# Output projections of a two-block transformer, divided along the contraction

## The chip, the cores and the metric

One core of a Trainium2 chip runs the whole program. The metric is the device time of one execution in microseconds (us). The engines are named as in the profile: PE is TensorE (matmul), PEld its weight load, DVE is VectorE, ACT is ScalarE, POOL is GpSimd, SP is SyncE.

## The reference

256 tokens of width 1024 go through four layers. All weights are float32 and are read once. The part that matters here is how each layer's attention output gets to its output projection:

```python
# first block, two layers
q, k, v, qi, ki, wi, u, vs = split(x @ w_in[i])
a_out = dsa_attention(...)            # top-64 keys chosen by an index score, 8 heads of 64 -> 512 columns
b_out = gelu(u) * (w_s @ layer_norm(gelu(vs)) + b_s)           # "gating", 512 columns
x = layer_norm(ALPHA * x + concatenate([a_out, b_out]) @ w_o[i])
# ... then ple gate, SwiGLU feed-forward, layer_norm

# second block, layer 0 (even) and layer 1 (odd)
o = concatenate([o_a, o_b])   # even: MLA 512 + dilated 256 columns; odd: differential 512 + MoBA 512
x = x + g1 * (o @ w_out)      # then rms_norm, modulate, squared-relu MLP, x + g2 * ...
```

## The kernel before

The 256 tokens are two tiles of 128 (`t` = 0, 1). A weight matrix comes in as a row of items of up to 128x2048 elements (1 MB); an item of 1024 rows x 512 columns is four contraction blocks of 128 rows. SP loads items into three buffers `RAW`; ACT rounds an item into `WH` and DVE subtracts to get `WL` (a **split**, done by `advance()`, at most `NPAIR` = 3 split items ahead of the items used up). The activations are turned on PE and split in the same way into `XTH`/`XTL` (`to_XT`, `turn_halves`: transposes on PE, then ACT writes XTH, then DVE writes XTL). A product is then three matmuls of 128x512 for each block (lines 1355 to 1357), so one whole item costs 12 matmuls for each token tile.

The order of work is written out once, as a list of parts (`do(...)`), and each engine runs its own share of every part strictly in the order of that list. A part that has to wait on an engine therefore holds up every later part on that engine. `busy(b, n)` (line 1340) puts `n` bf16 matmuls of 128x512 whose result is thrown away (**pads**) in front of a part; `pad`, `pads` and `first` set their number.

`attention(units, scale, filler, steps, pads, first)` runs over units of a few heads. Step k issues the scores of unit k, the transposes of unit k-1 (2 pads ahead unless said otherwise), then `steps[k]` pieces of a generator `filler`, then the products with the values for unit k-2. Softmax lies between: DVE reduces, ACT takes exponentials.

Before the attention of the first block stands the **selection**: PE index scores, then eight rounds on DVE (`sel_round`: MAX8 and MATCH_REPLACE8 for both tiles, lines 1834 and 1837) and the mask `selb` (line 1844), for which the first scores wait. In between, `next(fill)` issues the four items of `w_in` that give u and vs. They run on PE beside the rounds, in the order u, vs; ACT applies gelu into `GB`. After the last round comes `sgu_ln`, the layer norm of vs: two sums and two squares on ACT, small steps on POOL, two applications on ACT, then two multiplications and two additions of 128x512 on POOL (lines 1307 and 1311). The gating (8 matmuls and 4 DVE operations for each of two halves, lines 1411 and 1907, with a mask of the weights on DVE, line 1899) is a filler of the first three steps of the attention.

The output projection: in the attention, as soon as the attention output of tile 0 is ready, all of its 1024 (even layer: 768) columns are turned, and tile 0 is multiplied with the first 512 output columns. Then `guard` holds the rest until the attention is over. The other three of the four products (column half c, tile t) follow with the full contraction: (0,1), (1,0), (1,1). Behind each, DVE adds it to X (`residual`, or `gated_put`, two operations). The first block then normalises (`ln_tile`: statistics on DVE, two small steps on POOL, two operations on DVE) and runs `w_ple` and `w_ple_gate`; the second does `norm_tile` (ACT, POOL, DVE) and `go(t)` (8 transposes, modulation on ACT and DVE, split) before `mlp_w1`, which stands behind 11 pads.

Of the kernel before, what the change touches and what calls it, by code (L numbers as in the profile page):

```python
# [22 lines left out]
ALPHA = 4 ** 0.25  # L23
# [20 lines left out]
def plan():  # L44

    out = []

    def all_rows(name, i, k, *cuts):
        for cols in cuts:
            out.append((name, i, (0, k), cols if isinstance(cols, list) else [cols]))  # L50
# [18 lines left out]
    for i in range(2):  # L69
        if i == 0:  # L70
# [6 lines left out]
            all_rows("even_w_out_2", 0, 768, *halves)  # L77
        else:
# [3 lines left out]
            all_rows("odd_w_out_2", 0, 1024, *halves)  # L82
# [92 lines left out]
def program(nc, W, xd, xTd, pTd, posd, pos2d, colvd, cstd, cstbd, vecd, sgwd, smalld, out):  # L175
    with ExitStack() as ctx:
# [72 lines left out]
        def stationary(name, kt, t):  # L249
            if name == "x":  # L250
                return XTH[:, kt, tok(t)], XTL[:, kt, tok(t)]
            if name == "p":
                return PTH[:, kt, tok(t)], PTL[:, kt, tok(t)]
# [175 lines left out]

        def run(gen):  # L430
            for _ in gen:
                pass
# [57 lines left out]
        def to_XT(src, n, after, t, pad=0):  # L490
            return turn_halves([src[:, t, k * 128:k * 128 + 128] for k in range(n)], after, XTH, XTL, t, pad)
# [122 lines left out]
        def ln_tile(key, t, after, between=None):  # L614
            sts, mv = col(12), col(2)
            do("ln_stats", key, t, sts, mv, after)
            do("rsqrt", ("ln", key), mv[:, 1:2], 1.0, 1e-5, ("ln_mv", key))
            if between:
                between()
            do("ln_apply", key, t, mv)  # L620
            return [("ln", key)]
# [31 lines left out]
        for i in range(2):  # L653
# [21 lines left out]
            gw = [[], []]  # L675

            def gelus():
                for c in range(2):
                    def put(t, b, done, c=c):
                        do("gelu", (i, c, t), t, c, b, [done] + gb_free)  # L680
                        gw[t].append(("gelu", (i, c, t)))
                        give(b, gw[t][-1])
                    yield from linear("w_in", "x", xt_w, put)

            fill = gelus()
# [19 lines left out]
            for rnd in range(8):  # L705
# [4 lines left out]
                if rnd % 2:  # L710
# [4 lines left out]
            do("sgu_ln", i, gw, [col(1) for _ in range(2)], [col(1) for _ in range(2)], [col(1) for _ in range(2)],  # L715
               list(sq["free"]))
            sq["free"] = [("ln_ss", (i, 1))]
            vsw = [("sgu_ln", (i, t)) for t in range(2)]
# [23 lines left out]
            def gating():  # L742
                yield
                do("sgw_mask", i)
# [1403 lines left out]
```

How the kernel before makes its waits and increments, by code:

```python
    def wait_ge(self, sem, value):  # L169
        if self.past.get(id(sem), 0) < value:
            self.eng.wait_ge(sem, value)
            self.past[id(sem)] = value
# [1066 lines left out]
        def sync_program(eng):  # L1239
            on = Waits(eng)
            def load(n):
                it = seq[n]
                w = it["n"] * it["w"]
                if n >= NRAW:
                    on.wait_ge(*at(*seq[n - NRAW]["freed"]))
                eng.dma_start(RAW[:, n % NRAW, 0:w], W[it["off"]:it["off"] + 128 * w].rearrange("(p w) -> p w", p=128)
                              ).then_inc(*landed(f"raw{n % NRAW}", n))
            for n in range(NRAW):
                load(n)
            eng.dma_start(X[:, :, :], xd[0].rearrange("(t p) d -> p t d", p=128)).then_inc(*landed("x", 0))
            for n in range(NRAW, len(seq)):
                load(n)
            for part, args in order:
                if part == "store":
                    t, after = args
                    for e in after:
                        on.wait_ge(*at(*e))
                    eng.dma_start(out[0, tok(t), :], X[:, t, :]).then_inc(*landed(f"out{t}", 0))
            for t in range(2):
                on.wait_ge(*at(f"out{t}", 0))
# [11 lines left out]
            def rsqrt(key, x, scale, eps, summed):  # L1274
                on.wait_ge(*at("cst", 0))
                on.wait_ge(*at(*summed))
                eng.tensor_scalar(x, x, scale, eps, ALU.mult, ALU.add).then_inc(*own.up())
                on.wait_ge(*own.at())
```

## Time and profile before

| | |
|---|---|
| time, median of 3 runs | 1501.52 us (1497.39 to 1505.88) |
| the profiled execution | 1503.37 us, of which the span (first to last instruction) 1501.6 us |
| mean granted PE clock | 0.968 of 2.4 GHz |
| PE busy | 1414.2 us (94%) |
| DVE busy | 949.5 us (63%) |
| ACT busy | 657.9 us (44%) |
| POOL busy | 108.9 us (7%) |
| DMA | 269.87 MB, mean 180 GB/s |
| chain that ended last, by engine | PE 77%, DVE 13%, ACT 4%, issue 3%, DMA 2%, POOL 2% |

Times inside the profile are in us from the span's start. "Busy" counts an engine's own instructions, pads included. A matmul's duration overlaps the next one, so what a run of matmuls costs is the distance between their starts. The granted clock is a share of 2.4 GHz: 1.00 is 2.4 GHz, 0.50 is 1.2 GHz.

### The profile page before, as it was taken

What the parts mean: (1) busy time and instruction counts of PE and PEld (TensorE: products, weight loads), DVE (VectorE), ACT (ScalarE), POOL (GpSimd) and SP (SyncE); (2) the same over time, 40 slices, a digit from 0 to 9 for tenths busy, and PEclk for the clock granted to TensorE, in tenths of its full rate; (3) what the DMA queues carried; (4) which work ended last, traced back from release to release, by engine and by line L of the source; (5) the groups of instructions that cost most, each with busy time, mean ns of one, the idle gap of its engine ahead of it and who ended that gap; (6) DMA issues with size and microseconds to landing.
All of it is one profiled execution on the core that took longest, in us unless ns stands there. A gap on an engine that the chain in (4) does not pass through costs nothing.

```text
span 1501.6 us, 16677 instructions
## 1 busy us (share of the span) xinstructions
PE 1414.2 (94%) x6765; PEld 1140.7 (76%) x6765; DVE 949.5 (63%) x1239; ACT 657.9 (44%) x886; POOL 108.9 (7%) x156
## 2 busy tenths in 40 slices
PE   6999999999998999998799898999998998899998
PEld 6767888887867888886789666788876666688886
DVE  4856777766756677765586636766665775544444
ACT  4544533333554443433455334454435434355442
POOL 1010000001020000000222200000003120000000
PEclk9989999999999999999999869999999998999999
DMA  8504688863613688872243104677763330345451
GB/s 331 189 15 188 225 294 300 296 234 128 228 41 134 228 311 293 284 272 77 102 168 113 43 0 162 247 279 261 260 219 132 120 112 1 123 161 186 177 194 56
DMA packets 40236, 269.87 MB, mean 180 GB/s; under 512 B 4544, under 2 KB 4688, under 8 KB 11872
## 3 DMA queue, kind: packets, MB, share of 16 engines
q1 hardware_dynamic: 37712, 259.31, 48.2%
q0 software_dynamic: 2304, 8.46, 1.6%
q8 instruction: 53, 0.87, 0.2%
q10 hardware_dynamic: 144, 1.05, 0.2%
q14 instruction: 23, 0.19, 0.0%
HBM read 267.75 MB, written 1.05 MB: 179 GB/s over the span
## 4 chain that ended last, share of the span: by engine, by line
PE 77%; DVE 13%; ACT 4%; issue 3%; DMA 2%; POOL 2%; SPq 0%; POOLq 0%; DVEq 0%; ACTq 0%
PE ps L1355 21%; PE ps L1357 20%; PE ps L1356 20%; PE ps L1380 4%; PE ps L1432 4%; DVE WL L1662 3%; DMA RAW<-W 2%; PE ps L1447 2%; PE ps L1340 2%; ACT WH L1460 1%; PE ps L1368 1%; PE ps L1434 1%; POOL st L1279 1%; DVE SCR L1837 1%; DVE st L1924 1%
## 5 line engine op out<-in xcount | busy, mean ns | idle before, releaser
L1662 DVE TENSOR_TENSOR WL<-RAW,WH 128x2048 fp32r<-128x2048 f32 (+5 forms) x210 | 453.3, 2161 | 279.9 <-ACT WH L1460 279.7
L1355 PE MATMUL ps<-WH,XTH 128*128 128x512 f32 (+3 forms) x1176 | 460.6, 392 | 32.7 <-DVE XTL L1667 14.0
L1460 ACT ACTIVATE WH<-RAW 128x2048 fp32r<-128x2048 f32 (+5 forms) x210 | 379.9, 1810 | 247.0 <-PE ps L1357 219.5
L1357 PE MATMUL ps<-WH,XTL 128*128 128x512 f32 (+3 forms) x1176 | 449.3, 382 | 0.0
L1356 PE MATMUL ps<-WL,XTH 128*128 128x512 f32 (+3 forms) x1176 | 448.4, 381 | 0.0
L1355 PEld LDWEIGHTS ps<-WH,XTH 128*128 128x128 f32 x1176 | 223.7, 190 | 76.3 <-DVE XTL L1667 14.2
L1357 PEld LDWEIGHTS ps<-WH,XTL 128*128 128x128 f32 x1176 | 223.4, 190 | 38.8
L1356 PEld LDWEIGHTS ps<-WL,XTH 128*128 128x128 f32 x1176 | 223.7, 190 | 37.0 <-issue 1.9
L1355 PE MATMUL ps<-WH,HTH 128*128 128x512 f32 (+1 forms) x452 | 179.6, 397 | 3.2 <-DVE HTL L1743 3.2
L1356 PE MATMUL ps<-WL,HTH 128*128 128x512 f32 (+1 forms) x452 | 178.7, 395 | 0.0
L1357 PE MATMUL ps<-WH,HTL 128*128 128x512 f32 (+1 forms) x452 | 178.6, 395 | 0.0
L1721 DVE SCALAR_TENSOR_TENSOR ACC<-RAW,colv,ACC 128x512 f32<-128x512 f32 x168 | 126.1, 751 | 5.1
L1355 PEld LDWEIGHTS ps<-WH,HTH 128*128 128x128 f32 x452 | 85.9, 190 | 22.8 <-DVE HTL L1743 3.7
L1460 ACT ACTIVATE HTH<-ps 128x512 fp32r<-128x512 f32 (+1 forms) x58 | 32.1, 586 | 160.5 <-PE ps L1380 160.3
L1357 PEld LDWEIGHTS ps<-WH,HTL 128*128 128x128 f32 x452 | 85.9, 190 | 19.7
L1356 PEld LDWEIGHTS ps<-WL,HTH 128*128 128x128 f32 x452 | 86.1, 190 | 19.2
L1277 POOL TENSOR_SCALAR st<-st 128x1 f32<-128x1 f32 (+3 forms) x42 | 21.6, 514 | 1073.0 <-DVE st L1927 547.2
L1460 ACT ACTIVATE E<-ps,st 128x128 f32<-128x128 f32 (+1 forms) x104 | 42.5, 419 | 112.0 <-DVE st L1866 112.0
L1460 ACT ACTIVATE GB<-ps 128x512 f32<-128x512 f32 (+1 forms) x94 | 46.4, 499 | 88.3 <-PE ps L1357 88.1
L1340 PE MATMUL ps<-cstb 128*128 128x512 bf16 x283 | 81.7, 412 | 0.0
L1432 PE MATMUL ps<-T 64*128 64x128 f32 (+3 forms) x208 | 71.4, 435 | 8.7 <-DVE selb L1844 4.4
L1743 DVE TENSOR_TENSOR HTL<-ps,HTH 128x512 fp32r<-128x512 f32 x54 | 35.8, 687 | 37.7 <-ACT HTH L1460 37.7
(175 smaller groups left out, 1124.0 us busy)
## 6 DMA issues: line engine op xcount, KB each, us to landing
RAW<-W SPq DMA_DIRECT2D x220, 1024.0 KB, 4.8
RAW<-W SPq DMA_DIRECT2D x7, 960.0 KB, 4.7
RAW<-W SPq DMA_DIRECT2D x6, 910.0 KB, 5.8
RAW<-W SPq DMA_DIRECT2D x9, 576.0 KB, 3.5
VEC<-vecd POOLq DMA_DIRECT2D x10, 512.0 KB, 6.1
RAW<-W SPq DMA_DIRECT2D x8, 512.0 KB, 3.3
RAW<-W SPq DMA_DIRECT2D x6, 546.0 KB, 4.3
GB<-xTd ACTq DMA_DIRECT2D x1, 1024.0 KB, 8.4
```

Of the source, the lines that this page charges most:

```text
L1277: eng.tensor_scalar(x, x, scale, eps, ALU.mult, ALU.add).then_inc(*own.up())
L1340: eng.matmul(banks[b][:, :], identb, cstb[:, 0:512], start=True, stop=True)
L1355: eng.matmul(ps, xh, hi[:, j, c0:c0 + cw], start=first and j == 0, stop=False)
L1356: eng.matmul(ps, xh, lo[:, j, c0:c0 + cw], start=False, stop=False)
L1357: op = eng.matmul(ps, xl, hi[:, j, c0:c0 + cw], start=False, stop=last and j == n - 1)
L1380: op = eng.transpose(banks[b][0:rows, j * 128:j * 128 + 128], src, ident)
L1432: op = eng.matmul(banks[b][:, c:c + nk], q, ks, start=True, stop=True)
L1447: op = eng.matmul(banks[b][:, c0:c0 + dv], PET[:, u["i"], blk * 128:blk * 128 + 128], val, start=(j == 0), stop=(j == len(lst) - 1))
L1460: return eng.activation(dst, src, f, **k)
L1662: eng.tensor_tensor(WL[:, p, 0:w], RAW[:, n % NRAW, 0:w], WH[:, p, 0:w].bitcast(F32), ALU.subtract).then_inc(*up("wl", n))
L1721: op = eng.scalar_tensor_tensor(out=ACC[:, a, :], in0=view[:, j, :], scalar=cond[:, kt:kt + 1], in1=ACC[:, a, :], op0=ALU.mult, op1=ALU.add)
L1743: eng.tensor_tensor(HTL[:, r2:r2 + 2, :], banks[b][:, :].rearrange("p (n q) -> p n q", n=2), HTH[:, r2:r2 + 2, :].bitcast(F32), ALU.subtra ...
```

## The change

The contraction of every output projection is cut in two halves, each with its own item order in `plan()` and its own evacuation. In the first block, half one is the gating's 512 columns; in the second it is the 512 columns of the attention that ran earlier. Its four products are fillers of the attention from the second step on. The other half is done for tile 0 inside the attention, and for tile 1 behind it. Each of the four (c, t) results is therefore added to X twice: `residual` and `gated_put` run 8 times in a layer, not 4.

So that the gating's columns are there when the attention starts, vs comes before u in `w_in`, `sgu_ln` is divided in three parts (`sgu_sum`, `sgu_square`, `sgu_ln`), and mask and gating are pieces of the same filler as the gelus, of which now every round but the first takes one, not every second. The statistics of tile 0's layer norm are taken inside the attention. The pads change: 8 ahead of the first unit's transposes in the first block become 3, `first` in its second layer becomes 6.

```diff
@@ plan()
-        all_rows("w_in", i, 1024, (0, 364), (364, 728), (728, 1092), (1092, 1604), (1604, 2116))
-        all_rows("w_o", i, 1024, *halves)
+        all_rows("w_in", i, 1024, (0, 364), (364, 728), (728, 1092), (1604, 2116), (1092, 1604))
+        some_rows("w_o", i, 512, 1024, *halves)
+        some_rows("w_o", i, 0, 512, *halves)
...
-            all_rows("even_w_out_2", 0, 768, *halves)
+            some_rows("even_w_out_2", 0, 0, 512, *halves)
+            some_rows("even_w_out_2", 0, 512, 768, *halves)
...
-            all_rows("odd_w_out_2", 0, 1024, *halves)
+            some_rows("odd_w_out_2", 0, 0, 512, *halves)
+            some_rows("odd_w_out_2", 0, 512, 1024, *halves)
@@ new
+        def slots(its, lhs, after, evac, steps, pad=0):
+            for c, t in steps:
+                advance()
+                it, (b, fr), g = its[c], take(), uid()
+                do("mm", it, t, lhs, [(b, 0, it["w"], (g, t))], True, True, after[t], fr, 0 if c else pad)
+                if t:
+                    cur["used"] += 1
+                evac(c, t, b, ("mm", (g, t)))
+                flush()
+                yield
@@ first block, selection
             def gelus():
-                for c in range(2):
...
-                    yield from linear("w_in", "x", xt_w, put)
-
-            fill = gelus()
+                yield from gelu(1)
+                do("sgu_sum", i, gw, sgu[0], list(sq["free"]))
+                yield
+                second = gelu(0)
+                next(second)
+                do("sgu_square", i, sgu[0], sgu[1], sgu[2])
+                sq["free"] = [("ln_ss", (i, 1))]
+                yield
+                run(second)
+                do("sgu_ln", i, sgu[1], sgu[2])
+                do("sgw_mask", i)
+                yield
...
+            def gating():
+                for gh in range(2):
+                    b, fr = take()
+                    do("gating", i, gh, b, vsw + fr)
+                    give(b, ("gated", (i, gh)))
+                    yield
+
+            fill = chain(gelus(), gating())
...
-                if rnd % 2:
+                if rnd:
                     next(fill, None)
@@ first block, attention and behind it
             def out_start():
+                for t in range(2):
+                    mg[t][:] = to_XT(MIX, 8, [sgo], t, k0=4)
+                yield
+                yield from slots(two("w_o"), "x4", mg, put_gated, ((0, 0), (0, 1), (1, 0), (1, 1)))
                 while "out" not in keys_[0]:
                     yield
-                mo[0][:] = to_XT(MIX, 8, [keys_[0]["out"], sgo], 0)
+                mo[0][:] = to_XT(MIX, 4, [keys_[0]["out"]], 0)
                 yield
-                yield from linear("w_o", "x", mo, put_o(0), touter=True, guard=lambda: tail["go"], pad=(0, 3),
-                                  mid=lambda: mo[1].extend(to_XT(MIX, 8, [keys_[1]["out"], sgo], 1, pad=3)))
-
-            fill = chain(gating(), out_start())
-            attention(units, 0.125, fill, pads=(8,), first=8 if i else 3)
+                its_o.extend(two("w_o"))
+                yield from slots(its_o, "x", mo, put_o, ((0, 0), (1, 0)))
+                ln.append(ln_start((i, 1, 0), 0, rw[0]))
+                yield
+            fill = out_start()
+            attention(units, 0.125, fill, (1, 1, 2, 1, 1, 1, 1, 1), pads=(3,), first=6 if i else 3)
...
-            run(linear("w_o", "x", mo, put_o(1), touter=True,
-                       mid=lambda: x_n.__setitem__(0, ln_tile((i, 1, 0), 0, rw[0]))))
+            x_n[0] = ln_end(*ln[0])
+            mo[1][:] = to_XT(MIX, 4, [keys_[1]["out"]], 1, pad=3)
+            run(slots(its_o, "x", mo, put_o, ((0, 1), (1, 1)), pad=3))
+            xt_n[0][:] = to_XT(X, 8, x_n[0], 0)
             x_n[1] = ln_tile((i, 1, 1), 1, rw[1])
@@ second block, attention and behind it
             def out_start():
+                for t in range(2):
+                    xo[t][:] = to_XT(MIX, 4, [keys_[t]["out"]], t)
+                yield
+                yield from slots(two(nm_out), "x", xo, put_1, ((0, 0), (0, 1), (1, 0), (1, 1)))
                 while "out" not in keys_[2]:
                     yield
...
+                xo2[0][:] = to_XT(MIX, n_out, [keys_[2]["out"]], 0, k0=4)
                 yield
...
+                its_o.extend(two(nm_out))
+                yield from slots(its_o, "x4", xo2, put_2, ((0, 0), (1, 0)))
...
-            attention(units, 0.125, fill, first=3 if i else 0)
+            attention(units, 0.125, fill, (1, 1, 2, 1, 1, 1, 1, 1) if i else 1, first=3 if i else 0)
...
+            norm_tile(0, xg[1][0])
+            xo2[1][:] = to_XT(MIX, n_out, [keys_[3]["out"]], 1, pad=2, k0=4)
+            rest = slots(its_o, "x4", xo2, put_2, ((0, 1), (1, 1)), pad=3)
+            next(rest)
+            go(0)
+            run(rest)
+            norm_tile(1, xg[1][1])
```

## Rows read from the trace of the kernel before

**Rows 1.** Page, section 5: DVE's half of a split; busy, mean ns | idle before, releaser.

```profile
L1662 DVE TENSOR_TENSOR WL<-RAW,WH 128x2048 fp32r<-128x2048 f32 (+5 forms) x210 | 453.3, 2161 | 279.9 <-ACT WH L1460 279.7
```

**Rows 2.** Waits of PE: engine, line, releaser: us in total, times, longest.

```profile
PE ps L1380 <- DVE MIX L1942: 11.0, 5, 3.7
...
PE ps L1432 <- DVE selb L1844: 4.4, 2, 2.7
```

**Rows 3.** Windows: length, busy (x count) of PE, PEld, DVE, ACT, POOL, PEclk, DMA share, GB/s.

```profile
72.80:85.00 12.20, 12.17 (x44) 7.63 (x44) 4.87 (x7) 7.53 (x23) 7.09 (x9) 0.58 0.02 8
85.00:108.30 23.30, 23.30 (x143) 17.97 (x143) 12.12 (x24) 8.33 (x22) 0.00 (x0) 1.00 0.07 23
...
418.90:429.80 10.90, 10.86 (x45) 6.93 (x45) 5.21 (x7) 7.46 (x23) 7.08 (x10) 0.69 0.05 18
...
858.00:890.00 32.00, 32.00 (x112) 20.69 (x112) 9.10 (x30) 8.29 (x35) 0.00 (x0) 0.50 0.00 1
890.00:904.10 14.10, 14.10 (x96) 11.71 (x95) 6.78 (x11) 5.28 (x12) 0.00 (x0) 1.00 0.14 38
...
1249.30:1262.00 12.70, 12.70 (x47) 8.02 (x47) 4.91 (x10) 4.52 (x21) 1.21 (x2) 0.60 0.00 1
```

**Rows 4.** Timeline, first layer's selection and gating: start, us, engine, line, operation [idle before].

```profile
72.83 0.48 PE L1432 MATMUL ps<-T 64*128 64x128 f32 x2 [2.74 <-DVE selb L1844]
...
56.56 0.62 DVE L1834 MAX8 st<-SCR 128x8 f32<-128x128 f32 x2
...
57.74 0.61 DVE L1834 MAX8 st<-SCR 128x8 f32<-128x128 f32 x2
...
80.42 1.22 DVE L1899 TENSOR_TENSOR T<-T,cst 128x1024 f32<-128x1024 f32 x1
...
85.18 1.13 DVE L1907 SCALAR_TENSOR_TENSOR MIX<-ps,colv,GB 128x128 f32<-128x128 f32 x4 [3.55 <-PE ps L1411]
...
69.47 0.60 ACT L1460 ACTIVATE GB<-ps 128x512 f32<-128x512 f32 x1 [2.12 <-PE ps L1357]
...
74.83 2.49 POOL L1307 TENSOR_TENSOR GB<-GB,VEC 128x512 f32<-128x512 f32 x2
77.28 2.94 POOL L1311 TENSOR_TENSOR GB<-GB,VEC 128x512 f32<-128x512 f32 x2
```

**Rows 5.** Timeline of PE, first layer: pads, turned output, matmuls of w_o, gate.

```profile
79.37 3.62 PE L1340 MATMUL ps<-cstb 128*128 128x512 bf16 x8
...
109.52 1.09 PE L1380 MATMUL ps<-cst,MIX 128*128 128x128 f32 x8 [0.37 <-DVE MIX L1893]
...
112.27 0.47 PE L1355 MATMUL ps<-WH,XTH 128*128 128x512 f32 x1 [1.02 <-DVE XTL L1739]
...
115.11 0.39 PE L1355 MATMUL ps<-WH,XTH 128*128 128x512 f32 x1
...
117.83 0.39 PE L1355 MATMUL ps<-WH,XTH 128*128 128x512 f32 x1
...
142.64 0.50 PE L1355 MATMUL ps<-WH,XTH 128*128 128x512 f32 x1 [1.11 <-DVE WL L1662]
```

**Rows 6.** Timeline of DVE, first layer: layer norm of tile 1.

```profile
135.31 1.28 DVE L1924 BATCH_NORM_STATS2 st<-X 128x6 f32<-128x512 f32 x2
...
139.10 1.28 DVE L1937 SCALAR_TENSOR_TENSOR X<-X,st,VEC 128x1024 f32<-128x1024 f32 x1
```

**Rows 7.** Groups of PE by form in the even layer's attention, 855:890, then 890.1:905.

```profile
L1432 PE MATMUL ps<-T 64*128 64x256 f32 x18 | 11.0, 710 | 0.0
...
L1432 PE MATMUL ps<-T 64*128 64x256 f32 x6 | 2.1, 428 | 0.0
```

**Rows 8.** Timeline of PE, even layer: mlp_w1 starts, tile 1 is turned.

```profile
927.21 0.49 PE L1355 MATMUL ps<-WH,XTH 128*128 128x512 f32 x1 [2.89 <-DVE XTL L1768]
...
932.17 1.09 PE L1380 MATMUL ps<-cst,MIX 128*128 128x128 f32 x8
```

More of the change, by code:

```diff
@@ L488, in turn_halves, with to_XT @@
             return outs
-        def to_XT(src, n, after, t, pad=0):
-            return turn_halves([src[:, t, k * 128:k * 128 + 128] for k in range(n)], after, XTH, XTL, t, pad)
+        def to_XT(src, n, after, t, pad=0, k0=0):
+            return turn_halves([src[:, t, k * 128:k * 128 + 128] for k in range(k0, n)], after, XTH[:, k0:n, :],
+                               XTL[:, k0:n, :], t, pad)
         def col(n):
@@ L674, in program, with gelu, put @@
             do("load_vec", i, 1, VEC[:, 1024:2048], vb + 1024, vec_free[1])
-            gw = [[], []]
-            def gelus():
-                for c in range(2):
[L679 to L682, printed above, removed]
-                    yield from linear("w_in", "x", xt_w, put)
-            fill = gelus()
+            gw = []
+            sgu = [[col(1) for _ in range(2)] for _ in range(3)]
+            def gelu(c):
+                def put(t, b, done):
+                    do("gelu", (i, c, t), t, c, b, [done] + gb_free)
+                    if c:
+                        gw.append(("gelu", (i, c, t)))
+                    give(b, ("gelu", (i, c, t)))
+                return linear("w_in", "x", xt_w, put)
+            def gelus():
+                yield from gelu(1)
[10 more added lines that the diff above has]
+                yield
+            vsw = [("sgu_ln", (i, t)) for t in range(2)]
+            sgo = ("gated", (i, 1))
+            def gating():
[5 more added lines that the diff above has]
+            fill = chain(gelus(), gating())
             for t in range(2):
@@ L740, in program @@
                                           blocks=[c * 128 for c in range(per * (t + 1))]))
-            def gating():
-                yield
-                do("sgw_mask", i)
-                for gh in range(2):
-                    b, fr = take()
-                    do("gating", i, gh, b, vsw + fr)
-                    give(b, ("gated", (i, gh)))
-                    yield
-            sgo = ("gated", (i, 1))
             rw = [[], []]
             x_o, x_n = x_w, [None, None]
-            mo = [[], []]
@@ L885, in gain, with gated_put @@
             give(b, ("gain", g))
-        def gated_put(layer, c, k, xg):
-            def put(t, b, done):
-                do("gated_put", (layer, k, c, t), t, c, k, b, [done] + vg_w[k] + (xo_w[t] if k == 0 else []), x_w[t])
-                vg_free[k] = [("gp", (layer, k, c, t))]
-                xg[t].append(("gx", (layer, k, c, t)))
-                give(b, ("gp", (layer, k, c, t)))
-            return put
+        def gated_put(layer, k, buf, xg, c, t, b, done, after, x_after):
+            key, v = (layer, k, c, t), k // 2
+            do("gated_put", key, t, c, v, buf, b, [done] + vg_w[v] + after, x_after)
+            vg_free[v] = [("gp", key)]
+            xg[t].append(("gx", key))
+            give(b, ("gp", key))
         def put_H(name, c, a, b_, lst):
@@ L1214, in last @@
                 for c in range(2):
-                    gated_put(i, c, 1, xg)(t, acc4[t][c][0], done[c])
+                    gated_put(i, 2, MIX, xg, c, t, acc4[t][c][0], done[c], [], x_w[t])
                 if t:
```

96 lines of the change are left out of this document (50 added, 46 removed).

## The prediction

> **What bounds the kernel now.** I read four views, in this order. The page first: PE is busy for 94% of the span and 77% of the chain that ended last is PE, so the question for every edit is what PE waits for and what it does that is no work. The waits of PE say where it stands idle: behind MIX of the second block's norms, and for the selection mask [rows 2]. The windows of the stages this change touches are the most telling. In all of them PE is busy in practically every microsecond, through the softmax too, so there is no hole in the attention into which matmuls could be put for nothing [rows 3]. And they show the granted clock: 0.58 and 0.69 where the first block's attentions begin, 0.50 for 32 us in the even layer's attention, 0.60 where the odd one's begins. Last the timelines, for the order on each engine.
>
> **What is moved, and its price.** Twelve 128x512 matmuls, one item for one tile, cost 2.72 us at 2.4 GHz (117.83 less 115.11) [rows 5], 0.227 each. Of the 96 matmuls of an output projection 24 run in the attention now and 72 behind it; after the change it is 72 and 24. That is 48 matmuls or 10.9 us from one side to the other, in the even layer 42 or 9.5 us. As PE has no hole, I count this as neutral. Gains and losses are in the waits, the pads and the clock.
>
> **First block, selection: +9.5 us in each of two layers.** The gating now stands in the order in front of round 6, and its DVE half in front of rounds 6 and 7, so DVE cannot finish the selection before PE has done the gating, and PE cannot before POOL has normalised vs. Taken by the first layer:
> - ACT still does the gelus of the last item (now u) when PE ends it, 69.47 and 0.60 [rows 4]. `sgu_ln` stands behind them on ACT: two operations, the first done at about 70.8.
> - POOL then has its four operations, 2.49 + 2.94 us for the pairs [rows 4], or 4 x 1.25 = 5.0 if the additions are not disturbed. It ends at 75.9 to 76.3.
> - DVE reaches the gating after the weight mask (1.22) and round 5, near 71.5 (a round is 57.74 less 56.56, 1.18) [rows 4], and stands still.
> - PE's half of the gating takes 1.4 us at 1.2 GHz (PE idle by then for 6 us), DVE's 1.13, then round 6 (1.18), the second gating (1.13), round 7 (1.18) and the mask (0.3): 76.0 + 1.4 + 0.2 + 4.9 = 82.4. The scores began at 72.83 [rows 4]. Behind the waiting DVE instruction are queued the two last rounds and the mask; behind PE's are all scores.
>
> Bounds: 8.5 (POOL undisturbed, gating at 2.4 GHz) to 11. The removal of 2.3 us of gating from the attention is counted below. The sums and squares, done earlier, cost nothing: ACT waits for PE there.
>
> **First block, up to the third unit's scores: +4 and +5 us.** Now 12.2 and 10.9 us [rows 3]. Eight pads (3.4 from 79.37 on, at 1.2 GHz [rows 5]) and half of the gating (1.4) go. Three pads (1.3), eight transposes at 1.2 GHz (1.7) and 12 matmuls come. After an idle time of nearly 10 us with only the gating in it PE starts at 1.2 GHz, in the second layer too, so scores that ran fast cost 1 and 2 us more. What brings the clock back? Before, it was back within 5 us of the first of the 8 pads; I take the same from the new pads and matmuls on, so 12 matmuls cost 4.7. That gives 16.1 in both. Bounds: -3 (never cold) to +6.
>
> **First block, rest of the attention: +6.9 us each.** This stretch has 24 matmuls of w_o now and 60 then: +36, or +8.2; less the second half of the gating (0.9) and 4 transposes (0.4). The 23.3 us [rows 3] become 30.2. The extra DVE work (four residuals of 0.7, two turned halves, two splits of 2.2 [rows 1]) lies beside: DVE is busy for 12.12 of 23.3 us [rows 3]. Uncovered, it would cost 2 us in a step.
>
> **First block, behind the attention: -10.4 and +0.5 us each.** Now from 108.3 to the last matmul of w_o: PE waits until 112.27 (4.0) and does 72 matmuls (16.3), 20.3 in all [rows 5]. After: the transposes start as now (109.52), half of them, but on DVE the two operations of tile 0's norm (1.28 each [rows 6]) stand ahead of XTL, so PE starts at 4.4, and 24 matmuls end at 9.9. Behind it `slots` has no closing `advance()`: the first item of w_ple_gate is split on DVE behind the norm of tile 1. XTL of X at 2.6, the norm as now from 135.31 to 140.38 (5.1) [rows 6], the split 2.2: at 9.9. PE has only 6.3 us of work until then and stands for 3.6; then 12 matmuls, 4 pads and 8 transposes to 14.4, against 14.0 now (to 142.64 [rows 5]).
>
> One layer of the first block: 9.5 + 4 (5) + 6.9 - 10.4 + 0.5, about +10.5 and +11.5, **+22 us**.
>
> **Even layer: -13 us.** In its attention PE ran at 1.2 GHz for 32 us without a pause [rows 3]. The same scores cost 710 ns there and 428 ns behind it [rows 7], so this stretch is 0.6 as long at 2.4 GHz, or, with the pads and transposes, which halve, 0.57. The change puts 12 dense matmuls into the second step, about 858, and 24 more behind them. If they act like the pads of the first block [rows 5], the clock is up at 863; what came before from 856.6 on (34.8 us up to the last but two steps) then takes 19.6. Added are 30 matmuls more (6.8). The attention ends near 902, where it was 904.1: -2, with 42 matmuls more in it. Behind it 28.1 us pass until tile 1 is turned (932.17) [rows 8]. After: 2.2 until PE has XTL, 6 matmuls, 8 transposes, whose modulation takes some 6.3 as now (its end is the wait until 927.21 [rows 8]), so `mlp_w1` starts at 10.0. Then DVE has a split (2.2) ahead of the last `gated_put`, which it had behind it before, so tile 1 follows after 7.2 and not 5.0 [rows 8]: 17.2, -10.9. Bounds of this layer: -18 to +9, the latter if the clock stays down.
>
> **Odd layer: +0.6 us.** The clock is low for 10 us [rows 3] in both. Attention +10.9, and 0.4 for transposes. Behind it I take the even layer's 28.1 and 17.2 and add the matmuls that its narrower contraction spares, 18 (4.1) now and 12 (2.7) then, of which 0.5 is covered by waits: 32.2 less 19.4, and as the even layer waits longer for its own norm I count -12.2. PE then stands for 4 us ahead of tile 1's transposes, for which I charge 1.5, as of 3 us at half the clock.
>
> **Sum.** 22 - 13 + 0.6 = +9.6, on the profiled execution's 1503.4: 1513. That execution is 1.9 above the median, so the median should be **1511 us**.
>
> **A rule of the Trainium skill.** The rows first: PE was busy for 32.00 of 32 us at 0.50 [rows 3]. "TensorE: Matmul & The Clock Gate", section "What's actually happening", says that the clock is set by how busy PE has been, and that "the default state is throttled, and activity releases the throttle". By that rule, read with the profile's busy time, the 32 us should not exist, and a run in which they don't would leave nothing to gain; the trace disagrees, so what counts is not busy time as the page of the profile gives it. Rival three is this case.
>
> **The rivals.**
> - One, the selection is not held up, because vs is ready when DVE comes to it. For it: the sums and squares are earlier. Against it: POOL's 5 us cannot begin before ACT's last gelu [rows 4]. Without the 19 us the time is 1492.
> - Two, the first block's clock comes back with the eight transposes or is not lost. Less 9: 1502. For it: the clock stayed at 2.4 GHz in the rest of these attentions with few matmuls [rows 3].
> - Three, the even layer stays at 1.2 GHz, or would have lost its slow stretch anyway. For it: 12 matmuls are less than what else runs there. Then its matmuls cost double as well: up to +21, 1532. If the stretch is just not regained by change, +12, 1523.
> - Four, the in-order queues of ACT and DVE: splits and additions stand ahead of the softmax of the next unit. About 4.5 us of cover lie between a unit's scores and its transposes; a split on both engines takes 4.1. If one step in each layer is short by 2 us, +8: 1519. It decides from the point at which a split waits for matmuls of the same step.
>
> **How the numbers follow.** Forecast 0.50, rival one 0.14, two 0.13, three 0.08, four 0.15. The forecast's own spread is 6 us either way, from the bounds of POOL and clock. The range 1493 to 1524 leaves out most of rival one's lower half and of rival three. A measurement here can tell 0.5%, 7.5 us, from no change: under 1494 is faster, over 1509 slower. The forecast lies 2 us over the line, so of its 0.50 I give 0.31 to slower, 0.18 to the same, 0.01 to faster; with rivals three and four 0.54 slower, with two 0.31 the same, with one 0.15 faster.
>
> **What would show it.** In the changed kernel's trace: DVE idle for some 6 us ahead of line 1907's successor in the selection, released by PE; the scores of the first layer starting at 82 and not 73; the first block's attention from scores to last value 42 us and more; the even layer's attention at 1.00 from about 863 on; a wait of PE for WL ahead of w_ple_gate, and one of 4 us ahead of tile 1's transposes in both layers of the second block. It is wrong if the gating runs on PE before 74, if the even layer stays at 0.50, or if PE waits inside the attentions.

## The result, and the profile after

| | before | after |
|---|---|---|
| median | 1499.64 us (1497.39 to 1505.88, 4 runs) | 1522.56 us (1521.14 to 1524.35, 4 runs) |
| ratio | 1 | 1.0147, 95% interval 1.0112 to 1.0182 |
| the profiled execution | 1503.37, span 1501.6 | 1523.32, span 1521.5 |
| mean granted PE clock | 0.968 | 0.963 |
| PE busy | 1414.2 | 1413.2 |

The kernel is slower by 1.5%, some 20 us in span. The forecast was slower, 1511 in a range of 1493 to 1524: the sign held, and the loss was twice what the sum gave. A second set of runs of the same kernel gave 1.0171 (1.0121 to 1.0222).

PE was busy for as long as before (1413.2 us against 1414.2), and it stood still for 108.3 us of the span where it had stood for 87.4. That is the whole difference in the profile, but equal busy time doesn't mean equal work at an equal clock: by the mean clocks some 16 us more of the span lay at 1.2 GHz, and the kernel has 12 matmuls fewer (6753 against 6765). Waits of PE in the kernel after (engine, line, releaser: us in total, times, longest), answering [rows 2]:

```profile
PE ps L1446 <- DVE MIX L2011: 15.5, 5, 4.2
...
PE ps L1477 <- POOL GB L1376: 13.5, 2, 6.9
...
PE ps L1421 <- DVE WL L1731: 7.0, 3, 3.4
```

The first line is `norm_tile`'s MIX, 11.0 before. The second is new: the gating stands 6.7 and 6.9 us and waits for POOL. The third is the split item of `w_ple_gate`. The selection of the first layer, in timelines (start, us, engine, line, operation, idle before), answering [rows 4]:

```profile
76.04 3.76 PE L1477 MATMUL ps<-GB,T 128*128 128x128 f32 x16 [6.66 <-POOL GB L1376]
...
82.89 0.79 PE L1498 MATMUL ps<-T 64*128 64x128 f32 x2 [1.81 <-DVE selb L1913]
...
66.77 2.28 DVE L1731 TENSOR_TENSOR WL<-RAW,WH 128x2048 fp32r<-128x2048 f32 x1
68.97 1.22 DVE L1968 TENSOR_TENSOR T<-T,cst 128x1024 f32<-128x1024 f32 x1
...
78.19 1.13 DVE L1976 SCALAR_TENSOR_TENSOR MIX<-ps,colv,GB 128x128 f32<-128x128 f32 x4 [6.83 <-PE ps L1477]
79.24 0.61 DVE L1903 MAX8 st<-SCR 128x8 f32<-128x128 f32 x2
...
66.74 3.86 POOL L1363 TENSOR_TENSOR st<-st,cst 128x1 f32<-128x1 f32 x1
70.68 0.19 POOL L1365 TENSOR_TENSOR st<-st 128x1 f32<-128x1 f32 x1
70.86 2.49 POOL L1372 TENSOR_TENSOR GB<-GB,VEC 128x512 f32<-128x512 f32 x2
73.31 2.47 POOL L1376 TENSOR_TENSOR GB<-GB,VEC 128x512 f32<-128x512 f32 x2
```

Read it upwards: POOL ends at 75.78, PE's gating starts at 76.04, DVE, which has done nothing since 71.36, goes on at 78.19 with the gating and only then with round 6, and the first scores come at 82.89 instead of 72.83. Windows of the attentions (length, busy of PE, PEld, DVE, ACT, POOL, PEclk, DMA share, GB/s), answering [rows 3]:

```profile
82.90:97.70 14.80, 14.80 (x51) 10.29 (x52) 4.44 (x9) 6.27 (x20) 0.00 (x0) 0.57 0.01 1
97.70:127.90 30.20, 30.20 (x167) 23.41 (x167) 15.98 (x24) 8.89 (x22) 0.00 (x0) 1.00 0.25 87
442.60:456.40 13.80, 13.80 (x52) 9.63 (x52) 4.21 (x9) 6.27 (x20) 0.00 (x0) 0.63 0.01 1
...
879.00:927.90 48.90, 47.15 (x279) 35.42 (x280) 27.11 (x64) 18.54 (x63) 0.00 (x0) 1.00 0.17 59
927.90:948.20 20.30, 14.25 (x55) 8.70 (x53) 10.15 (x17) 8.96 (x13) 1.50 (x4) 0.83 0.18 67
1267.40:1311.20 43.80, 43.35 (x216) 32.60 (x217) 25.79 (x37) 16.13 (x42) 1.20 (x2) 0.88 0.19 66
```

The even layer's attention (879.00 on) is at 1.00 throughout, where 32 us of it were at 0.50 in [rows 3]. Ahead of tile 1's transposes behind it, and in the odd layer too (4.20), PE waits for the norm:

```profile
948.20 1.26 PE L1446 MATMUL ps<-cst,MIX 128*128 128x128 f32 x8 [4.22 <-DVE MIX L2011]
```

What lies behind the first attention, on PE, answering [rows 5]:

```profile
129.57 0.66 PE L1446 MATMUL ps<-cst,MIX 128*128 128x128 f32 x4 [0.83 <-DVE MIX L1962]
...
133.00 0.64 PE L1421 MATMUL ps<-WH,XTH 128*128 128x512 f32 x1 [2.13 <-DVE XTL L1808]
140.17 1.03 PE L1446 MATMUL ps<-cst,X 128*128 128x128 f32 x8
150.06 0.58 PE L1421 MATMUL ps<-WH,XTH 128*128 128x512 f32 x1 [3.40 <-DVE WL L1731]
```

The table has the gains and losses by stage, each the difference of the two traces' distances between the same two events. It compares one execution of each kernel, and between executions of one kernel a stage can move by several us with the clock, as a second trace of the kernel after shows below.

| stage | forecast | measured |
|---|---|---|
| first block, to the first scores | +9.5, +9.5 | +10.1, +10.1 |
| to the third unit's scores | +4, +5 | +2.6, +3.0 |
| to the last value product | +6.9, +6.9 | +6.9, +6.9 |
| behind the attention, up to the next layer's scores or (second layer) the scores of the even layer's second attention | -9.9, -9.9 | -6.1, -5.1 |
| even layer, attention | -2 | -4.6 |
| even layer, to the turned tile 1 | -10.9 | -7.7 |
| from there to the odd layer's first scores | 0 | +2.1 |
| odd layer, attention | +11.3 | +11.8 |
| odd layer, to the turned tile 1 | -10.7 | -11.3 |
| from there to the end | 0 | +1.3 |
| sum | +9.6 | +20 |

### The profile page after: what moved, and what is told of

Same layout as the page of the kernel before. It is cut to its first block, busy times and chain, and to the rows that moved or that the text cites. A ratio compares the mean times of both kernels' runs of the same rounds, so it can differ in the third digit from the quotient of the medians.

```text
span 1521.5 us, 16700 instructions
## 1 busy us (share of the span) xinstructions
PE 1413.2 (93%) x6753; PEld 1142.1 (75%) x6753; DVE 962.1 (63%) x1263; ACT 656.7 (43%) x886; POOL 119.8 (8%) x156
## 4 chain that ended last, share of the span: by engine, by line
PE 76%; DVE 11%; ACT 4%; issue 3%; POOL 3%; DMA 2%; SPq 0%; POOLq 0%; DVEq 0%; ACTq 0%
PE ps L1421 21%; PE ps L1423 21%; PE ps L1422 21%; PE ps L1446 4%; PE ps L1498 3%; DVE WL L1731 2%; DMA RAW<-W 2%; ACT WH L1526 1%; PE ps L1406 1%; PE ps L1434 1%; PE ps L1500 1%; POOL st L1340 1%; PE ps L1513 1%; DVE st L1993 1%; DVE X L2003 1%
## 5 line engine op out<-in xcount | busy, mean ns | idle before, releaser
L1421 PE MATMUL ps<-WH,XTH 128*128 128x512 f32 (+3 forms) x1176 | 467.6, 398 | 36.1 <-DVE XTL L1736 15.0
L1406 PE MATMUL ps<-cstb 128*128 128x512 bf16 x271 | 77.0, 405 | 0.0
L1498 PE MATMUL ps<-T 64*128 64x128 f32 (+3 forms) x208 | 65.0, 402 | 7.3 <-DVE selb L1913 3.1
```

The source lines that it names most:

```text
L1406: eng.matmul(banks[b][:, :], identb, cstb[:, 0:512], start=True, stop=True)
L1421: eng.matmul(ps, xh, hi[:, j, c0:c0 + cw], start=first and j == 0, stop=False)
L1498: op = eng.matmul(banks[b][:, c:c + nk], q, ks, start=True, stop=True)
```

## The experiments

The theory that went into them: the loss is made in the first block, by the order (gating in front of the last rounds on DVE; norm of tile 0 in front of the turn, and the split behind the norm of tile 1), and each wait of PE costs more than its length, since the clock is at 0.50 behind it. The rivals: the divided contraction itself costs (more evacuations, more queueing), or the loss is the second block's.

**The new selection alone, in the kernel before.** vs first, `sgu_ln` in three parts, mask and gating among the rounds; everything else as before.

```diff
+            fill = chain(gelus(), gating())
...
-                if rnd % 2:
+                if rnd:
                     next(fill, None)
...
-            fill = chain(gating(), out_start())
+            fill = out_start()
```

> The kernel before with the changed selection alone: vs ahead of u, sgu_ln in three parts, mask and gating as pieces between the rounds. The output projections are undivided, the attention and its pads as before. Theory (the gating in front of rounds 6 and 7 delays the first scores by 10 us in each layer and takes 2.3 us out of the attention, with a few us more at 1.2 GHz): +17 to +22, about 1519. Rival (the delay only shows because divided matmuls follow it): under 1508.

Measured: 1517.23 (1516.21 to 1517.88), ratio 1.0136 (1.0086 to 1.0185), so +17.3 by the medians. PE of this kernel, first layer:

```profile
76.11 3.76 PE L1428 MATMUL ps<-GB,T 128*128 128x128 f32 x16 [6.66 <-POOL GB L1328]
...
82.97 0.49 PE L1449 MATMUL ps<-T 64*128 64x128 f32 x2 [1.82 <-DVE selb L1863]
```

The wait is the same to the hundredth. No contraction is divided here, so the order of the selection makes a loss by itself, and not because divided matmuls follow it. How much of the whole it is depends on what it is set against. From the first layer's index scores (PE at 51.2 us in all three traces) to the even layer's second attention the kernel before takes 799.4 us, this kernel 14.4 more and the kernel after 28.5 more. So the selection is half of what the first block loses; the other half is the divided contraction there, whose attentions grow by more than its tails shrink. The +17.3 of this kernel look like more of the changed kernel's +22.9 because the latter has the even layer's gain in it.

**The reverse: only the gating moved back.** The kernel after, with mask and gating in the attention's filler.

```diff
-                do("sgw_mask", i)
                 yield
...
             def gating():
+                do("sgw_mask", i)
                 for gh in range(2):
...
-            fill = chain(gelus(), gating())
+            fill = gelus()
...
-            fill = out_start()
-            attention(units, 0.125, fill, (1, 1, 2, 1, 1, 1, 1, 1), pads=(3,), first=6 if i else 3)
+            fill = chain(gating(), out_start())
+            attention(units, 0.125, fill, (2, 1, 2, 2, 1, 1, 1, 1), pads=(3,), first=6 if i else 3)
```

> The changed kernel with one thing moved: the mask of the gating's weights and the gating itself are no longer pieces of the selection's filler, they are the first two pieces of the attention's filler. The divided contraction stays. My theory (the gating holds up the selection's last rounds on DVE, 10.1 us in each first-block layer): the first layer's scores start at 73 and not 82.9, the gating's 2.3 us of PE come back into each attention, and less time at 1.2 GHz gives some 4 us: about 1503 (1499 to 1508) against 1522.6. Rival (the loss comes from the matmuls that were moved into a PE without a hole, or from the order of ACT and DVE in the attention): 1517 or more.

Measured: 1508.9 (1504.19 to 1512.05), ratio 1.0068 (1.0032 to 1.0104); 13.7 us came back of the some 19 expected. The first scores stand at 73.79 again. What can be seen of the rest: the two gating pieces fell into the first step and met the mask there:

```profile
79.45 3.78 PE L1477 MATMUL ps<-GB,T 128*128 128x128 f32 x16 [2.11 <-DVE T L1968]
```

PE waits 2.11 us for the mask of the weights, the 16 matmuls take 3.78 us at the low clock, and the clock stays at 0.50 for 17.1 us from 74.2 on, against 10.2 in the kernel before. (By the traces 11.8 of the first block's 28.5 us came back.)

**PE kept busy through the wait.** The kernel after with 28 pads ahead of the first gating and 16 instead of 3 and 6 ahead of the first scores. The order, and so the wait, stay.

```diff
             def gating(i, gh, b, after):
+                if gh == 0:
+                    for e in after[2:]:
+                        on.wait_ge(*at(*e))
+                    busy(b, 28)
...
-            attention(..., pads=(3,), first=6 if i else 3)
+            attention(..., pads=(3,), first=16)
```

> The changed kernel with PE kept busy while it waits in the selection: 28 pads ahead of the first gating and 16 pads ahead of the first scores, in both layers. The waits stay, only what PE does in them is another. It prices the clock alone. Theory (of the first block's loss, the 24 and 17 us at 1.2 GHz cost some 6 us a layer, and the gating gets 1 us shorter): -10 to -14, 1508 to 1513 against 1522.6. Rival (the stall is the whole loss): 1518 to 1523.

Measured: 1512.0 (1510.92 to 1516.16), ratio 1.0107 (1.0055 to 1.0158), 11 us less than after. The first scores are hardly earlier (82.58), but the gating is faster, and so are the attentions:

```profile
76.65 2.02 PE L1481 MATMUL ps<-GB,T 128*128 128x128 f32 x16 [0.52 <-POOL GB L1376]
```

and by windows, the two attentions of the first block (45.0 and 44.0 us in the kernel after):

```profile
82.60:125.30 42.70, 42.54 (x215) 32.06 (x219) 20.63 (x32) 15.17 (x42) 0.00 (x0) 0.92 0.18 62
438.50:478.20 39.70, 39.54 (x215) 30.21 (x219) 20.25 (x32) 15.04 (x42) 0.00 (x0) 1.00 0.20 67
```

By the medians of four executions each, pads that compute nothing gave 11 us back of 22.9, so about half of the kernel's loss was clock and not waiting. In the first layer the clock still fell at 85.2, for 6.8 us; in the second attention not at all. This second attention is no proof by itself, though. The kernel after was run again unaltered beside this one, with 1523.01 (1520.26 to 1523.63, 4 runs), and its profiled execution was its quickest. In that trace the two attentions are

```profile
83.70:127.85 44.15, 43.98 (x215) 33.16 (x219) 20.51 (x32) 15.16 (x42) 0.00 (x0) 0.88 0.17 60
443.80:483.40 39.60, 39.44 (x215) 30.17 (x219) 20.14 (x32) 15.04 (x42) 0.00 (x0) 1.00 0.20 67
```

so without any pad the second one took 39.6 us at 1.00, where it took 44.0 in the first profile of the same kernel. The clock in this stage changes from execution to execution, and what the pads gave rests on the medians.

**The tail repaired.** The kernel after, with the turn of tile 1 ahead of the norm of tile 0, and the closing `advance()` ahead of the norm of tile 1.

```diff
-            x_n[0] = ln_end(*ln[0])
             mo[1][:] = to_XT(MIX, 4, [keys_[1]["out"]], 1, pad=3)
+            x_n[0] = ln_end(*ln[0])
             run(slots(its_o, "x", mo, put_o, ((0, 1), (1, 1)), pad=3))
             xt_n[0][:] = to_XT(X, 8, x_n[0], 0)
+            advance()
```

> The changed kernel with two repairs behind the first block's attention: the turned MIX of tile 1 stands ahead of tile 0's norm on DVE, and a closing advance() splits the first item of w_ple_gate ahead of tile 1's norm. Theory (those two orders cost PE 1.1 and 3.4 us of waiting, and each wait is followed by 3.4 us at 1.2 GHz, which costs 1.7): between -2 and -5 us in each layer, 1513 to 1519. Rival (the norm behind the split comes as much later, as it did before): no difference, 1521 to 1524.

Measured: 1513.15 (1505.29 to 1515.7), ratio 1.0087 (1.0051 to 1.0123), 9.4 less than after, near the upper end of what was expected. PE, first layer:

```profile
130.38 0.50 PE L1422 MATMUL ps<-WH,XTH 128*128 128x512 f32 x1 [0.77 <-DVE XTL L1809]
...
149.07 0.50 PE L1422 MATMUL ps<-WH,XTH 128*128 128x512 f32 x1 [1.11 <-DVE WL L1732]
```

Waits of 0.77 and 1.11 stand where 2.13 and 3.40 stood, 3.65 us less, and no stretch at 0.50 is left behind either attention of the first block. One wait is new, for the norm of tile 1, now behind the split:

```profile
146.87 1.09 PE L1447 MATMUL ps<-cst,X 128*128 128x128 f32 x8 [0.81 <-DVE X L2007]
```

So PE stands 2.8 us less in a layer. From the pads behind the attention to the three pads in the middle of w_ple_gate the way is 5.8 us shorter in the first layer (33.79 to 27.98) and 5.7 in the second: the other half, some 3 us in a layer, is what the two stretches at 0.50 had cost. The traces' 11.5 us in both layers are more than the 9.4 of the medians.

**Both repairs together**, with the gating one step later (steps (0, 2, 2, 3, 1, 1, 1, 1)).

> The changed kernel with both repairs: mask and gating as fillers of the attention's second step, so that DVE and PE meet them later than in e1_gate_late, where PE stood 2.1 us for the mask; and the two orders behind the attention of e4_tail. Theory (the parts add up: -13.7 and -9.4 measured, and up to 2 us more in each layer for the mask): 1496 to 1500 against 1522.6 of the changed kernel, no better than the second block's part alone (1497.2), since moving matmuls in the first block gives nothing. Rival (the division gives something there once the stall is gone, as its design intends): under 1492.

Measured: 1501.59 (1496.36 to 1508.3), ratio 1.0031 (1.0 to 1.0061). 1.6 us above what was expected. The two repairs nearly add up (13.7 + 9.4, measured 21), and the kernel with the divided contraction is back where the kernel before was. It has not gained. That the two repairs take away what the one selection and the two orders had cost is the second proof of these causes, beside the selection put alone into the kernel before.

**The second block alone.** First block as before, second block changed.

> The kernel before with the second block's part of the change alone; the first block is as before, its selection, gating and tail too. Theory (the two blocks add up, the first costs some 28 us, the second gives some 9): about 1491 (1486 to 1495). Rival (the second block's gain in the one trace is the clock's chance in one execution): 1496 to 1502, no difference from the kernel before.

Measured: 1497.2 (1491.56 to 1500.75), ratio 0.9975 (0.9943 to 1.0007). A miss: 4 us and not 10, and no difference that can be told. By its trace the even layer behaves as in the kernel after (its second attention takes 49.1 us at 1.00, the part behind it 19.1). But this is the trace of its quickest execution, 1491.56, as forecast; six of its ten lie at 1497.0 to 1500.8 with a lower clock (0.971 to 0.976 against 0.979). The next run asks what gives the even layer its gain.

**The even layer's clock in the kernel before.** Nothing of the change; only 10 pads instead of 2 ahead of the transposes of the first unit in the even layer's attention.

```diff
-            attention(units, 0.125, fill, first=3 if i else 0)
+            attention(units, 0.125, fill, pads=() if i else (10,), first=3 if i else 0)
```

> The kernel before with 10 pads in place of 2 ahead of the first unit's transposes in the even layer's second attention, nothing else. It tells what gives the even layer's gain. Clock theory (dense matmuls early in that attention bring PE back to 2.4 GHz, and it stays there): 8 more pads cost 3.4 us, 27 us at 1.2 GHz become some 16, so -8: 1492 (1488 to 1496). Rival (the gain is the shorter tail, or the clock stays down as it did with 2 pads): +2 to +4, 1502 to 1504.

Measured: 1492.67 (1489.98 to 1499.01, 10 runs), ratio 0.9946 (0.9916 to 0.9976). Windows of the even layer, attention and then to the turned tile 1, first of the kernel before:

```profile
850.60:904.10 53.50, 53.46 (x232) 37.18 (x233) 18.16 (x51) 16.27 (x59) 0.00 (x0) 0.65 0.04 10
904.10:932.20 28.10, 23.11 (x101) 16.46 (x100) 17.75 (x24) 12.58 (x16) 2.29 (x4) 0.94 0.38 134
```

then of this kernel:

```profile
853.50:895.30 41.80, 41.80 (x241) 29.18 (x242) 17.89 (x51) 16.27 (x59) 0.00 (x0) 0.92 0.05 15
895.30:924.00 28.70, 23.70 (x98) 16.92 (x97) 18.50 (x25) 12.57 (x16) 2.29 (x4) 0.89 0.39 138
```

Eight pads, 3.4 us of work for nothing, shorten the attention from 53.5 to 41.8 us. So the even layer's gain needs no divided contraction. 41.8 + 28.7 = 70.5 here, 49.1 + 19.1 = 68.2 with the second block changed, and 3.4 of the 70.5 are the pads; whether the changed layer gains anything against one at the high clock is measured further down.

The kernel before does not always run with one clock either. Its 69 runs in these sessions lie in two groups: 50 between 1496.9 and 1509.5 at a mean granted clock of 0.960 to 0.971, and 19 between 1487.5 and 1493.4 at 0.975 to 0.979. The profiled execution (0.968) is one of the 50, and so are the four runs of the result. No trace of one of the 19 was taken, so that it is the even layer's slow stretch which they lack is only argued from the times: the medians of the groups lie 12.7 us apart, and the kernel with pads, where the stretch is down to 6.8 us, has nine of ten runs under 1497. The miss of the run before is not explained by the two groups: on that chip the median of all 31 runs is 1500.76 and that of the slower 23 is 1501.62, a shift of 0.9 us, where 6 are missing. The rest is in that kernel's own executions with a lower clock than the traced one; where they lose it no trace shows.

**Pads in the waits alone.** The kernel before, with the waits ahead of the first scores of the four attentions filled: the pads take time in which PE stood still. In the first block the run changes a second thing, the 8 pads ahead of the first unit's transposes become 2.

```diff
-            attention(units, 0.125, fill, pads=(8,), first=8 if i else 3)
+            attention(units, 0.125, fill, pads=(2,), first=16 if i else 15)
...
-            attention(units, 0.125, fill, first=3 if i else 0)
+            attention(units, 0.125, fill, first=12 if i else 4)
```

> The kernel before, in which the waits of TensorE ahead of the first scores are filled with pads that write a bank nobody reads: 15 and 16 pads instead of 3 and 8 in the first block's two layers, 4 and 12 instead of 0 and 3 in the second block's, and 2 pads instead of 8 later in the first block's attention. If the clock is what a wait costs beside its own length (the 10.2, 6.8, 37.5 and 10.2 us at 0.50 behind the first scores of the four attentions go), some 3 + 2 + 9 + 4 us come back and the time is 1480 to 1488. If the pads only take the place of waits and the clock falls later all the same, it is 1497 to 1503.

Measured: 1490.31 (1486.58 to 1492.14, 10 runs), ratio 0.9944 (0.9911 to 0.9978): the lowest median of the study, though not the 1480 to 1488 expected, and by the ratio not to be told from the kernel with pads in the even layer alone (0.9946). Windows of the first layer (the pads, the first 3 us of scores; then the whole attention in three parts), and of the even layer:

```profile
69.00:73.39 4.39, 4.24 (x20) 1.86 (x18) 4.39 (x15) 3.09 (x8) 0.71 (x4) 1.00 0.65 241
73.39:76.50 3.11, 3.10 (x17) 2.17 (x17) 0.15 (x1) 2.31 (x5) 2.79 (x6) 1.00 0.04 13
...
73.40:81.20 7.80, 6.40 (x27) 3.72 (x27) 4.44 (x7) 5.47 (x15) 7.05 (x9) 0.70 0.01 4
81.20:90.20 9.00, 9.00 (x32) 6.63 (x33) 2.71 (x7) 3.32 (x14) 0.00 (x0) 0.50 0.01 2
90.20:110.40 20.20, 20.20 (x125) 15.77 (x124) 10.13 (x18) 6.82 (x17) 0.00 (x0) 1.00 0.09 27
```

```profile
856.10:893.00 36.90, 36.90 (x234) 27.10 (x234) 17.51 (x51) 16.15 (x59) 0.00 (x0) 1.00 0.06 16
893.00:920.90 27.90, 22.91 (x99) 16.27 (x96) 17.71 (x24) 12.57 (x16) 2.30 (x4) 0.94 0.37 136
```

In the even layer 4 pads ahead of the scores are enough: 36.9 us at 1.00, 16.6 less than before (and a stretch of 6.8 us at 0.50 ahead of these scores, where there were 3.4). In the first block nothing was won (its attentions take 36.8 and 34.3 us, 35.5 and 34.2 before), and the first theory's reason falls there. PE had 4.24 of 4.39 us of pads and matmuls and 3.10 of 3.11 us of scores behind it, its longest pause being 0.15 us, and at 76.6 the clock fell all the same. So the wait ahead of the first scores is not needed for the fall: here it came 3.2 us into the scores without one. Behind it PE, ahead of the softmax now, waited for the exponentials:

```profile
81.17 1.11 PE L1380 MATMUL ps<-cst,E 128*128 128x128 f32 x4 [1.40 <-ACT E L1460]
```

and the clock was at 0.50 from 76.6 to 90.2, 13.7 us and not the 10.2 of before. Six of the 8 pads that had stood inside this stretch were gone, so the 13.7 do not measure the filled wait alone. (In the second layer and in the odd one it fell too, for 6.8 us each.) Both expectations were half right: in three attentions the clock fell all the same, in the even layer it did not. All ten runs lie at 1486.6 to 1492.1, where the 19 quick ones of the kernel before do (1487.5 to 1493.4).

**The same with 10 pads in the even layer.** The expectation speaks of each transpose step. The edit, `pads=() if i else (10,)`, puts the 8 more ahead of the first unit's transposes alone, as in the run above.

> The same with 10 pads instead of 2 ahead of each transpose step of the even layer's second attention. If the 4 pads ahead of its first scores already hold the clock, the 8 more per unit only cost time and this is 0 to 8 us slower than the kernel without them; if the clock falls there without them, this is the faster, 1480 to 1485.

Measured: 1492.07 (1489.15 to 1500.28), ratio 0.9968 (0.9933 to 1.0003). By its trace the even layer's second attention takes

```profile
857.40:896.00 38.60, 38.60 (x242) 27.99 (x242) 17.88 (x51) 16.27 (x59) 0.00 (x0) 1.00 0.05 15
```

1.7 us more than with 4 pads alone: the additional pads bring nothing, as by the first case, since the clock was already at 1.00. The 1.8 us between the medians are within the two kernels' spread.

**The divided contraction at an equal clock.** The kernel with both repairs and the same pads in the same waits (16 or 15 in the first block, 4 and 12 in the second).

> The repaired kernel after (gating inside the attention, the turn ahead of the layer norm) with the same pads in the same waits. If the divided contraction itself is neutral once no clock is lost, the time is that of the kernel before with these pads, 1480 to 1488, within 4 us of it. If the divided contraction gains behind the attention what was meant, it is 5 to 12 us below that kernel; if the gating in the attention's units costs more than the tail gives, 5 to 10 us above.

Measured: 1497.77 (1490.93 to 1503.55), ratio 1.0006 (0.9964 to 1.0048), on the same chip in the same rounds as the undivided kernel with pads, and 7.5 us above it. Their granted clocks are alike, 0.975 to 0.982 and 0.977 to 0.982, so in sum this difference is not clock: in the traces PE stands still for 93.1 us of the span and not 86.8. The even layer of this kernel:

```profile
855.50:904.50 49.00, 47.29 (x280) 35.43 (x280) 27.10 (x64) 18.68 (x63) 0.00 (x0) 1.00 0.17 61
904.50:924.70 20.20, 14.24 (x53) 8.72 (x51) 10.14 (x17) 8.86 (x13) 1.50 (x4) 0.83 0.17 63
```

Against the undivided one the attention is 12.1 us longer, of which 9.5 are the moved matmuls and 1.7 a wait that was not there (for PET, the turned softmax weights of a unit, which DVE copies); behind it 7.7 are saved and not 9.5, as PE stands for 4.19 us ahead of tile 1's transposes and 6.8 us of the 20.2 go at the low clock. By common events of the two traces: up to the even layer's second attention -0.6, from there to the odd layer's +6.4, the rest +1.2. Within a stage clock does play a part, and it cancels between them. Of the 6.4 about half is clock: PE has 6.8 us more at 0.50 there. On the way to the even layer's second attention this kernel has 13.7 us less at 0.50 than the undivided one, and is still only 0.6 ahead.

## Why the prediction was right, and where it was not

- **Selection, +9.5 each.** Right in mechanism and size: DVE idle 6.83 us ahead of the gating (forecast some 6), first scores at 82.89 (82.4). Shown by the selection put alone into the kernel before and by the gating moved back. One thing was not foreseen and cost nothing: POOL's power of one column (one element in each partition) took 3.86 us while DVE ran operations with two inputs, 0.56 otherwise. POOL waited with it anyway until ACT had applied the norm.
- **To the third unit, +4 and +5.** Measured +2.6 and +3.0, inside the bounds. The term rested on when the clock returns, and it returned earlier (at 0.50 from 71.8 for 23.9 us, so to 95.7, where some 97 was taken). That the second layer came so near the +5 is in part luck: in the trace of another execution of the same kernel it had its clock there, and the whole attention took 39.6 us and not 44.0.
- **Rest of the attention, +6.9.** To a tenth, in both layers: the 36 matmuls were the whole cost and the DVE work lay beside, so rival four did not occur in the first block. In the even layer it did once, a wait of 1.72 us for PET at 926.48.
- **Behind the attention, -9.9 each.** The term that was mis-sized: -6.1 and -5.1, of which 1.0 in the second layer falls only inside the second block, ahead of the even layer's second attention; the tails themselves are -6.1 in both. The waits were right (3.40 us for WL, 3.6 forecast) but I charged them by their length. Behind each, 3.4 us ran at 0.50 (from 133.2 and 150.3 in the first layer), at most 1.7 us more each time. PE's start was 5.1 and not 4.4 us behind the attention: DVE had the statistics of tile 0's norm in its queue ahead of it too. Together 4.1 us, where 3.8 are missing in each tail; with these waits cut the stretches at 0.50 were gone and 9.4 us came back. In the odd layer such a price had been charged (1.5), in these layers not.
- **Even layer, -13.** In sum nearly exact, -12.3, the clock at 1.00 from the first scores on and not only from some 12 us into it, which makes the -4.6 for the attention where -2 was forecast. But the price of the tail was the same error as above (-7.7 instead of -10.9, with 6.8 us at 0.50 from 928.5 on), so the near hit of the sum is two errors that cancel. And the gain doesn't need the change: 4 or 8 pads give it in the kernel before, and the times of 19 of 69 runs speak for its being there without any. Rival three named this, that the slow stretch would have gone anyway, with 1523 for it. The 1522.56 measured are no sign of it: the four runs they are compared with are all of the slower group, the even layer did gain its 12.3 us in the traces, and the loss beyond the forecast lies elsewhere.
- **Moved matmuls count nothing.** Right for PE's busy time (1414.2 and 1413.2). With pads in both kernels and alike mean clocks the divided form still cost 7.5 us, of which the traces put 6.4 between the even layer's second attention and the odd one's, where two waits are new (PET 1.7, MIX 4.2 us; PE stands 3.0 us longer in all) and 6.8 us more go at 0.50. That these are the whole of it was not tried by itself.
- **The rule on the clock.** The 32 us at 0.50 with PE busy throughout [rows 3] are not bound to this stretch: eight pads of 128x512 shortened them, four ahead of it took them away. The page "TensorE: Matmul & The Clock Gate" of the Trainium skill, section "What's actually happening", says that activity releases the throttle. The runs agree with it in that these pads brought the clock to 1.00 and PE kept it; but PE was busy by the profile for all of the 32 us too, so the busy share of a profile does not tell which it will be.

Of the sum's error of 10 us, the two tails of the first block are 7.6 and the way from the second to the even layer's second attention 1.0, the even layer's tail 3.2, what follows behind the two tails of the second block 3.4 and the selections 1.2; the stretches before the third unit gave 3.4 and the even attention 2.6 back, the odd layer 0.1. The mechanism was right in the selection and in the attentions; the price of a wait behind them was the step that was too small.

## What to carry to other kernels

Ahead of moving work to an earlier place, look at what stands behind it on each in-order queue: here 16 matmuls that waited for POOL held up the last rounds on DVE and with them every score. Price a wait of the engine that sets the end by its length and by the stretch at the low clock behind it: in the tails of this kernel, where products of 128x512 follow, up to 1.7 us for waits of 2 to 4 us and nothing for those of 0.8 to 1.1 us; ahead of scores it was more (2.74 us of waiting in the kernel before, then 10.2 us at 0.50). And before a gain in clock is credited to a change, put a few pads into the old kernel: here four shortened the even layer's second attention by 16.6 us, where the whole change gained 12.3 in that layer. One profile of a kernel is one execution of it: compare its time with the others before reading its clock.

## What was not expected of the hardware

- A stretch without a single pause of PE (32.00 of 32 us) ran at 1.2 GHz in both traced kernels that have it unchanged (before, and before with the new selection: 37.5 us each) and at 2.4 GHz with four pads of 128x512 ahead of it. What separates the 50 executions from the 19 of the same program is open.
- Scores (pairs of 64x128 with 64 rows of contraction) let the clock fall without a wait ahead of them: PE was busy for 7.34 of the 7.50 us from 69.00 on, and from 76.6 on ran at 0.50 for 13.7 us. In the even layer the same kernel's scores, behind 4 pads, did not. Why the one and not the other is open.
- One and the same kernel after had its second attention at 1.00 in one trace (39.6 us) and 10.2 us of it at 0.50 in another (44.0 us).
- POOL's power on 128x1 took 2.54 and 3.86 us beside DVE operations with two inputs in SBUF, ending 0.4 us behind them, and 0.56 to 0.67 alone. It is not the power: in the second layer it was the step ahead of it, otherwise 0.19 us, that fell beside DVE's split:

```profile
422.89 2.37 POOL L1361 TENSOR_SCALAR st<-st 128x1 f32<-128x1 f32 x1 [1.97 <-ACT SQ L1526]
...
426.26 3.51 POOL L1361 TENSOR_SCALAR st<-st 128x1 f32<-128x1 f32 x1
```

The Trainium skill, "SBUF — State Buffer", section "Who interferes with whom", has the two engines exclude each other on a shared pair of ports for a whole instruction. These rows agree in that POOL was done only behind DVE; in the 3.86 and 3.51 us it was behind two operations of DVE in a row, 2.28 and 1.22 us.
